# mLSTM stage of a two-layer hybrid block: where modulation sums, a head's norm and the layer norm's squares are worked

## The reference

```python
def even_mixer(h, hc, w_in, w_out, ...):
    p = h @ w_in                                   # and pc = hc @ w_in
    q, k, v, o, g = mlstm_inputs(p, gate_b)
    h_m, hc_m = bidir_mlstm(qc, kc, vc, gc, q, k, v, g)
    y = concat([conv_module(p[..., :2 * D_CONV], ...), mlstm_merge(h_m, o, norm_g)]) @ w_out

def conv_module(glu_in, dw_w, ln_g, ln_b):         # 31 taps, then a layer norm, then silu
    a, b = split(glu_in);  u = dwconv(a * sigmoid(b), dw_w)
    return silu(layer_norm(u, ln_g, ln_b))

def mlstm_merge(h, o, norm_g):                     # RMS norm of each head, times the output gate
    return rms_norm(h, norm_g) * sigmoid(o)
```

## Time and profile before

| | |
|---|---|
| median of three runs | 1645.91 us (1640.68 to 1647.05) |
| the profiled execution | 1644.94 us, its span 1643.2 us, mean granted clock 0.988 |
| busy: PE, PEld, DVE, ACT, POOL | 1602.0, 1346.5, 1022.0, 561.7, 18.1 us |
| taps on DVE, both loops | about 90 to 243 us |
| product `o` on PE, the conv mean in its middle | 251.3 to 273.7 us |
| the heads on PE | 273.7 to 372.7 us |
| `out0` on PE from | 372.7 us |

### The profile page before, as it was taken

One profiled execution on the slowest core, in us unless ns is written; L12 is line 12 of the kernel. 1 busy time (PEld: TensorE's weight loads), 2 busy tenths in 40 slices (PEclk: granted clock), 3 DMA queues, 4 the chain that ended last, 5 costly groups with the idle time before them and its releaser, 6 DMA issues.

```text
span 1643.2 us, 21952 instructions
## 1 busy us (share of the span) xinstructions
PE 1602.0 (97%) x8678; PEld 1346.5 (82%) x8678; DVE 1022.0 (62%) x1505; ACT 561.7 (34%) x896; POOL 18.1 (1%) x58
## 2 busy tenths in 40 slices
PE   6999999999999999999999999899999999999998
PEld 3888887778898888888888887788887988888886
DVE  4999992758847774577526437755876443354345
ACT  5323115465632221132211325523336332232233
POOL 0000000110000000000000000000000000000000
PEclk9999999989999999999999999999999999999999
DMA  9512121434126553445333231220012233223232
GB/s 314 180 28 77 55 75 46 135 103 116 32 73 225 196 178 104 143 164 180 114 97 122 53 101 52 88 96 27 1 31 86 73 94 116 90 90 112 79 97 83
DMA packets 134009, 169.43 MB, mean 103 GB/s; under 512 B 15970, under 2 KB 92450, under 8 KB 133930
## 3 DMA queue, kind: packets, MB, share of 16 engines
q1 hardware_dynamic: 133674, 168.25, 32.0%
q10 hardware_dynamic: 256, 0.08, 0.0%
HBM read 166.17 MB, written 2.15 MB: 102 GB/s over the span
## 4 chain that ended last, share of the span: by engine, by line
PE 91%; DVE 4%; ACT 3%; issue 1%; DMA 1%; SPq 0%; DVEq 0%; POOL 0%; ACTq 0%
PE acc L730 49%; PE acc L779 23%; PE acc L756 4%; PE acc L1191 2%; PE acc L971 2%; PE acc L1122 2%; PE acc L844 2%; PE acc L875 1%; PE acc L1006 1%; PE acc L1137 1%; PE acc L698 1%; DVE h_lo L1649 1%; DVE w_lo L1649 1%; PE acc L950 1%; DMA ada<-in_ada_w 1%
## 5 line engine op out<-in xcount | busy, mean ns | idle before, releaser
L730 PE MATMUL acc<-h_hi,w_hi 128*128 128x512 f32 (+1 forms) x1424 | 417.1, 354 | 4.9 <-DVE w_lo L1649 4.2
L730 PE MATMUL acc<-h_hi,w_lo 128*128 128x512 f32 (+1 forms) x1424 | 412.3, 350 | 0.0
L730 PE MATMUL acc<-h_lo,w_hi 128*128 128x512 f32 (+1 forms) x1424 | 412.1, 350 | 0.0
L1649 DVE TENSOR_TENSOR w_lo<-raw,w_hi 128x1024 fp32r<-128x1024 f32 x183 | 218.2, 1220 | 155.5 <-ACT w_hi L1211 155.3
L730 PEld LDWEIGHTS acc<-h_hi,w_hi 128*128 128x128 f32 x1424 | 230.7, 189 | 42.9 <-issue 5.3
L730 PEld LDWEIGHTS acc<-h_lo,w_hi 128*128 128x128 f32 x1424 | 230.7, 189 | 38.8 <-issue 0.5
L1211 ACT ACTIVATE w_hi<-raw 128x1024 fp32r<-128x1024 f32 x183 | 186.5, 1054 | 216.5 <-PE acc L779 169.9
L730 PEld LDWEIGHTS acc<-h_hi,w_lo 128*128 128x128 f32 x1424 | 229.7, 188 | 37.6
L779 PE MATMUL acc<-w_hi,hid_hi 128*128 128x512 f32 x440 | 175.0, 398 | 0.0
L779 PE MATMUL acc<-w_lo,hid_hi 128*128 128x512 f32 x440 | 174.4, 396 | 0.0
L779 PE MATMUL acc<-w_hi,hid_lo 128*128 128x512 f32 x440 | 174.4, 396 | 0.0
(11 more groups left out here) (267 smaller groups left out, 2057.9 us busy)
## 6 DMA issues: line engine op xcount, KB each, us to landing
ada_w<-in_ada_w SPq DMA_DIRECT2D x88, 512.0 KB, 5.9
raw<-in_ffn_w_in SPq DMA_DIRECT2D x88, 512.0 KB, 3.7
raw<-in_ffn_w_out SPq DMA_DIRECT2D x44, 512.0 KB, 4.2
raw<-in_even_w_in SPq DMA_DIRECT2D x24, 512.0 KB, 4.5
ada<-in_ada_w SPq DMA_DIRECT2D x8, 1024.0 KB, 11.8
raw<-in_odd_w_in SPq DMA_DIRECT2D x12, 512.0 KB, 4.2
raw<-in_even_w_out SPq DMA_DIRECT2D x8, 512.0 KB, 5.4
ada_m<-in_ada_w SPq DMA_DIRECT2D x8, 512.0 KB, 4.2
```

What stands on the lines that cost most here:

```text
L730: last = nc.tensor.matmul(acc[:, s, m, t0:t1], w[:, slot, kk, c], x_[:, k, t0:t1], start=(k == 0 and q == 0), stop=(k == KD - 1 and q == 2))
L1649: return nc.vector.tensor_tensor(out_, in0, in1, op)
```

## The change

- The 1024 columns of `ada_m` become two chunks, `EVEN[2]` and `EVEN[3]`. `EVEN[2]` is summed on DVE in two halves inside the second tap loop (at taps 8 and 16), its columns on PE follow the product `qkov[5]`. `EVEN[3]` is summed after `conv_done`; its columns (`last_columns`, 8 matmuls) come behind item (0, 2) on PE. `ada_m` with its transfers, waits and 128 records goes. On SP the loads of `EVEN[2]` stand ahead of the gates' granules, those of `EVEN[3]` ahead of granules 22 and 23; granules 28 and 29 are loaded after head 0's `negM`.
- The four tiles of squares are added on DVE into one (three additions), so that PE sums one tile. `unit_low(26)` comes after them.
- On ACT, the first exps of head 0 are made before and after the squares, and small activations on one column load the next function's table ahead of need.
- A head's norm is spread over the next head: squares at q = 1 as before, inverse at q = 2, root at q = 3, product at q = 4, turning and gating after q = 5. `head_out` stands after that on ACT, `head_low` at q = 1 of the head after the next on DVE; those of head 2 after the loop. `forward_sums` follows the gating.

```diff
-EVEN = [Chunk((0, 1), q, 0, 4 + q, 0) for q in range(2)]
+EVEN = [Chunk((0, 1), q, 0, 4 + q, 0) for q in range(4)]
...
-ITEMS += [("X", h - 1, 0) if q == "X" else ("S", h, q) for h in range(1, HEADS) for q in (0, 1, 2, "X", 3, 4, 5)]
+ITEMS += [("X", h - 1, 0) if q == "X" else ("S", h, q) for h in range(1, HEADS) for q in (0, 1, 2, 3, 4, 5, "X")]
...
             load_unit(sp, n + 6, w_even, 256)
+            load_ada(sp, 2, 0, 6)
...
                 load_unit(sp, G["qkov"] + 2 * j, w_even, 1024 + 256 * j)
+                if j == 5:
+                    load_ada(sp, 3, 0, 7)
             load_unit(sp, G["o"], w_even, 1024 + 256 * 7)
-            for k in range(4):
+            for k in range(2):
                 load_token(sp, "out0", w_even_out, 0, k)
...
                 if h == 1:
+                    for k in range(2, 4):
+                        load_token(sp, "out0", w_even_out, 0, k)
                     sp.wait_ge(sem("ln_var"), 1)
...
-                load_ada_m(h, h + 1)
...
-                product(pe, U["qkov"] + j, G["qkov"] + 2 * j, h, always)
+                product(pe, U["qkov"] + j, G["qkov"] + 2 * j, h, always, ada=EVEN[2] if j == 5 else None, of=sums_even[0])
...
+            def last_columns():
+
+                pe.wait_ge(ada_used, 4 * EVEN[3].seq + 8)
+                for q in range(4):
+                    for x_ in range(2):
+                        c = 944 + 2 * q + x_
+                        last = nc.tensor.matmul(acc[:, 0, 1, c:c + 1], sums_last[x_][:, q * P:(q + 1) * P], ones[:, 0:1],
+                                                start=False, stop=True, skip_group_check=True)
+                last.then_inc(sem("last_columns"), 1)
...
-                if pending:
+                if kind == "S" and pending:
                     if pending[1] == 0 and hd:
                         pe.wait_ge(sem("sums_taken_fwd"), hd)
                         pe.wait_ge(sem("sums_taken_rev"), hd)
                     weigh(*pending)
-                pending = (hd, q) if kind == "S" else None
+                if kind == "S":
+                    pending = (hd, q)
                 if not z:
-                    spread_sums(lambda t, t0, t1, c: ln_sq[t][:, t0:t1], 1, lambda t: pe.wait_ge(sem("ln_sq_ready"), t + 1)
-                                ).then_inc(sem("ln_var"), 1)
+                    pe.wait_ge(sem("ln_sq_summed"), 1)
+                    for t0, t1 in SEGS[T]:
+                        last = nc.tensor.matmul(acc[:, 1, 1, t0:t1], ones[:, :], ln_sq[0][:, t0:t1], start=True, stop=True)
+                    last.then_inc(sem("ln_var"), 1)
                     psum_free(pe, U["mlstm"] + 1)
-                if kind == "S":
-                    for part in ADA_PARTS.get((hd, q), ()):
-                        ada_part(hd, part)
+                if (kind, hd, q) == ("S", 0, 2):
+                    last_columns()
...
+            def load_table(f, c):
+
+                nc.scalar.activation(mark[:, c:c + 1], eps[:, 0:1], f)
...
+            psum_read(act, U["turned"])
+            sa.done(nc.scalar.activation(gcols[:, 2:4], gcols[:, 2:4], ACT.Exp, scale=-1.0))
+            exps(0, 0, 0, 3)
...
+            exps(0, 0, 3, 4)
+            load_table(ACT.Sigmoid, 12)
...
                     if q == 1 and hd:
-                        finish(hd - 1)
+                        head_squares(hd - 1)
                     if q == 3 and hd:
-                        head_out(hd - 1)
+                        head_root(hd - 1)
...
                                              ).then_inc(sem("sums_taken_rev"), 1)
+                        if hd:
+                            head_out(hd - 1)
...
+                    if (t, w) in ((2, 8), (2, 16)):
+                        ada_sums(EVEN[2], sums_even[0], first=0 if w == 8 else 4, end=4 if w == 8 else KD)
...
             nc.vector.tensor_copy(mark[:, 2:3], ident[:, 0:1]).then_inc(sem("conv_done"), 1)
-            unit_low(26)
+            ada_sums(EVEN[3], [x_[:, :] for x_ in sums_last])
...
+            for t in range(1, 4):
+                sd.wait()
+                dve.wait_ge(sem("ln_sq_ready"), t + 1)
+                ins = vt(ln_sq[0][:, :], ln_sq[0][:, :], ln_sq[t][:, :], ALU.add)
...
+            unit_low(26)
...
+            def head_end(z, hd):
+
+                if hd < HEADS - 1:
+                    dve.wait_ge(sem("slot_full"), z + 2)
+                    weighted(z + 1, hd + 1, 0, 0, 2)
+                forward_sums(hd)
...
                                                    qkov[:, 12 + hd, :], ALU.mult, ALU.mult).then_inc(sem("merged_ready"), 1)
+                    head_end(z, hd + 1)
                     continue
...
-                if q == 1 and hd:
+                if q == 1 and hd >= 2:
+                    head_low(hd - 2)
+                if q == 2 and hd:
                     head_inverse(hd - 1)
+                if q == 4 and hd:
                     head_normed(hd - 1)
...
+            head_low(last - 1)
             head_inverse(last)
```

More of the change, by code:

```diff
@@ L943, in _ @@
             last.then_inc(unit_done, 1)
[L945 to L952, removed]
             def conv_mean():
@@ L956, in conv_mean @@
                 pe.wait_ge(sem("conv_done"), 1)
-                spread_sums(lambda t, t0, t1, c: conv_t[t][:, c:c + t1 - t0], 0, always).then_inc(sem("ln_mean"), 1)
+                for t in range(4):
+                    for (t0, t1), c in zip(SEGS[T], (HALF, U_CTX)):
+                        last = nc.tensor.matmul(acc[:, 1, 0, t0:t1], ones[:, :], conv_t[t][:, c:c + t1 - t0],
+                                                start=(t == 0), stop=(t == 3))
+                last.then_inc(sem("ln_mean"), 1)
             product(pe, U["o"], G["o"], h, always, amid=conv_mean)
@@ L1437, in _, with exps @@
             unit_high(G["qkov"] + 2 * 6 + 4)
+            def load_table(f, c):
+                nc.scalar.activation(mark[:, c:c + 1], eps[:, 0:1], f)
+            def exps(hd, q, first, end):
+                if q == 0 and not first:
+                    act.wait_ge(sem(f"m_in{hd % 2}"), 16 * (hd // 2 + 1))
+                for e, (d, t0, t1) in STEPS[q][first:end]:
+                    if 16 * hd + e == 3:
+                        act.wait_ge(sem("conv_done"), 1)
+                    if 16 * hd + e >= 4:
+                        act.wait_ge(sem("p_used"), 16 * hd + e - 3)
+                    nc.scalar.activation(probs[e % 4][:, 0:t1 - t0], negM[:, hd % 2, d, t0:t1], ACT.Exp,
+                                         bias=gcols[:, d, ORDER[q], hd + 4 * d:hd + 4 * d + 1]).then_inc(sem("e_ready"), 1)
+            psum_read(act, U["turned"])
+            sa.done(nc.scalar.activation(gcols[:, 2:4], gcols[:, 2:4], ACT.Exp, scale=-1.0))
+            exps(0, 0, 0, 3)
             conv_segs = tuple(zip(SEGS[T], (HALF, U_CTX)))
@@ L1453, in conv_root @@
                 last.then_inc(sem("ln_rooted"), 1)
+                load_table(ACT.Exp, 14)
             def conv_silu(first):
@@ L1484, in head_out @@
                 nc.scalar.activation(h_hi[:, 4 + hd, :], merged[hd][:, :], ACT.Copy).then_inc(sem("mix_high"), 1)
-            def exps(hd, q, first, end):
-                if q == 0 and not first:
-                    act.wait_ge(sem(f"m_in{hd % 2}"), 16 * (hd // 2 + 1))
-                for e, (d, t0, t1) in STEPS[q][first:end]:
-                    if 16 * hd + e == 3:
-                        act.wait_ge(sem("conv_done"), 1)
-                    if 16 * hd + e >= 4:
-                        act.wait_ge(sem("p_used"), 16 * hd + e - 3)
-                    nc.scalar.activation(probs[e % 4][:, 0:t1 - t0], negM[:, hd % 2, d, t0:t1], ACT.Exp,
-                                         bias=gcols[:, d, ORDER[q], hd + 4 * d:hd + 4 * d + 1]).then_inc(sem("e_ready"), 1)
             for kind, hd, q in ITEMS:
                 if kind == "S":
-                    exps(hd, q, 2 if hd and not q else 0, 4)
+                    if hd or q:
+                        exps(hd, q, 2 if not q else 0, 4)
                     if (hd, q) == (0, 0):
```

81 lines of the change are left out of this document (31 added, 50 removed).

## The result

The changed kernel takes 1623.54 us, the median of four runs from 1622.82 to 1626.13; the kernel before took 1643.94 beside it (four runs, 1640.68 to 1647.05). The ratio is 0.9885, 95% interval 0.9869 to 0.9902. Measured two more times it is 0.9891 [0.9871, 0.9910] and 0.9893 [0.9872, 0.9914]. The forecast was 1624, so the time is met to half a microsecond. Part of that is luck. The forecast gain, 22.2 of 1645.91 us, is a ratio of 0.9865 and lies just outside the measured interval: by the ratio the gain is 18.9 us, at most 21.5. The 22.2 were subtracted from a median of three runs that lies 2 us above that of the four. The profiled execution takes 1623.9 us, its span 1621.9, mean granted clock 0.995.

What follows compares the result with a forecast made beforehand. TensorE, busy 97% of the span, bounds the kernel; the mLSTM stage holds removable work, waits and half-clock time. Terms 2.2 - 7.2 - 5.1 - 4.9 - 7.2 = -22.2 us take 1645.91 to 1624 us; range 1618 to 1634.

Steps and rivals of the forecast that it cites:

- A: Ahead of the heads: two more chunks on DVE cost PE +2.2 us, bounds 1.7 to 5.
- The cover: DVE's slack ahead of the heads: 2.8 + 3 us; whatever DVE loses beyond 6 us, PE loses too.
- the stall: PE's wait for unit_low(22) behind the columns of EVEN[2], near 231 us: 0.5 us.
- B: Head 0: squares summed on DVE, ada_m out, last_columns in, gaps closed: -7.2 us.
- C: Heads 1 to 3: norm spread off PE's path and ada_m gone: -5.1, -4.9 and -7.2 us.
- rival 1: Heads: clock falls all the same, from small PE gaps and thin work: +8.5 us, 1632; chance 0.13.
- D: Behind the heads: head_low(2) and head_out(2) move after head 3's sums: 0, up to +1 us.
- The table load: ACT's root at q = 3: load 1.28 us without the skill's 1.38 us drain, which would make 1632.
- The signs: Expected traces: clock 1.0 in heads, h_tok the stage's largest wait; w_lo wait over 1 us near 231 proves wrong.
- Slower (2): Heads: clock stays at its lower level throughout, up to 1689 us, half of it 1657; chance 0.03.
- The front (3): Ahead of the heads: granule 22 or the tap loop late, PE stalls 6.5 us, 1631; chance 0.07.
- Rival 4: Heads 1 to 3: den chain or DVE takes the norm's place, -6 instead of -17.2 us, 1635; chance 0.09.

Runs made afterwards that it cites:

- cover: Sixteen further 512-column DVE passes, results unused, put ahead of EVEN[3]'s sums in the changed kernel; one execution, 1627.59 us.
- norm_only: Kernel before with only the norm spread over the next head, ada_m and the four tiles of squares kept; 1635.26 us, ratio 0.9946.
- squares_4: Changed kernel with the four tiles of squares summed on PE again, without DVE's three additions; 1629.76 us, ratio 0.9915.
- norm_block: Changed kernel with the norm put back as one block behind q = 1, ada_m still gone; 1637.88 us, ratio 0.9977.
- late_out: Changed kernel with head_out moved behind the q = 0 exps of the head after the next, root still at q = 3; 1623.76 us, ratio 0.9890.
- no_den: Changed kernel with the denominators left out and ones in their place, so output is not the reference's; one execution, 1620.27 us.
- thin: Changed kernel with 16 two-column matmuls added at q = 2 of heads 1 to 3; 1633.91 us, ratio 0.9952.
- block_filled: Changed kernel with the norm as one block again, plus 18 unread 120-column matmuls a head where PE then idled; 1635.27 us, ratio 0.9958.

## Why the prediction came out, point by point

**A, +2.9 where +2.2 stood.** The terms that were there hold in this execution: 2.12 us from the columns of `EVEN[2]` at 229.88 to the next matmul at 232.00, that is 1.7 of columns and 0.4 of waiting for `w_lo` (forecast 1.7 and 0.5), no wait for granule 22, `conv_done` at 254.2 (253.9), centring from 268.1 (267.5). The rest stands ahead of the taps and is no effect of the change: the columns of `EVEN[1]` start at 82.47, 0.64 us later than in the kernel before, and in the two other traced executions of the changed kernel (one of each further measurement) at 81.52 and 80.88. Counted from those columns to the first scores A is 193.95 - 191.73 = 2.2 us, as forecast.

Two things in A need mending. The cover was mis-sized: 2.8 + 3 us stood, 3.10 + 0.84 are in the trace, and `cover` lost 3.15 us where 6 us of cover would have lost 1.4. And the stall is not fixed. In the traced execution of the third measurement (1624.85 us) PE comes to the columns of `EVEN[2]` 3.7 us earlier, `w_lo` from DVE only 1.6 us earlier, and PE waits 2.4 us (PE in order of time, and the stretch with the columns as above):

```profile
226.22 1.84 PE L685 MATMUL acc<-ones,ada_c 128*128 128x1 f32 x16
230.43 0.98 PE L717 MATMUL acc<-h_hi,w_hi 128*128 128x512 f32 x2 [2.38 <-DVE w_lo L1652]
```
```profile
227.00:237.00 10.00, 7.62 (x34) 6.61 (x34) 10.00 (x11) 4.04 (x8) 0.00 (x0) 0.66 0.35 107
```

The clock falls there as well. Its first scores come at 276.73 all the same. `norm_only`, whose work ahead of the heads is that of the kernel before, has them at 271.33, 2.2 us ahead of the kernel before, though its `EVEN[1]` columns start at 82.13. So A depends on how fast PE gets through its products: counted from the `EVEN[1]` columns it is 2.2 us between these two slower traces, and 195.85 - 189.20 = 6.7 us between these two faster ones, the wait and the lower clock included. That is more than the 5 that stood as its bound.

**B, -6.7 where -7.2 stood.** From the first scores: variance 1.3, weighing 0 at 2.6 (forecast 2.6), columns over at 11.5 (11.4), the last weighing over at 20.3 (19.8), head 1 at 22.35 (21.7). The 0.65 us that it is late are 0.05 to 0.2 at the hand-offs from one engine to another and 2.1 instead of 1.9 for the den chain; the length before, 29.04 in one view, was put at 28.9 by a start from the chain's. The largest single term, the squares, is confirmed by `squares_4`: 3.87 us. The other terms (`ada_m` out of head 0, `last_columns` in, gaps closed) were not tested singly.

**C, -16.8 where -17.2 stood.** Head by head the counting in pieces held to 0.6 us. Two reasons beside it need mending.

The sum is right, but it has no parts that can be had singly. Over the three heads `norm_block` gains 70.1 - 68.9 = 1.2 us, `norm_only` 6.6, both together 16.8: 9 us belong to neither alone. The ratios of the timed runs give less, 5 to 6 us: they make 3.8 us for `norm_block`, 8.9 for `norm_only` and 17.9 to 18.9 for the change, each known to about 3 us (A and B are in the first and the last). In the kernel before, the norm's chain and the `ada_m` piece lay beside each other, each about 4 us long. With either gone the other still holds PE for that time, once as idle time, once as thin work, and mostly with the slow matmuls behind it. Counting before and after as whole chains gave the right answer; adding up the edits would not have.

The clock's cause was put too narrowly. "Each fall comes on the heels of `ada_m`" was true of the rows, but `norm_block` shows the same fall behind 4.1 us of idle PE, so rival 1's premise (gaps lower it as well) holds for long gaps. It didn't come true in the heads: the gaps left there are 0.15 to 0.89 us, and behind those the clock stayed at 1.00 throughout. The rule of "TensorE: Matmul & The Clock Gate", section "A second HAM failure mode: psum-queue depth-cycling", in the Trainium skill (frequent short idles make the clock swing) is thus not borne out in these stretches.

Head 2's miss (18.65, not 18.1) has its place: the exps of q = 0 come late behind `head_out`. I had let `head_out` cost 0.5 us ahead of q = 1 and nothing inside the weighing of q = 0, which takes 2.97 us there instead of 2.72; `late_out` takes that quarter away and `no_den` shows the same engine next in line. The small waits at q = 1 and q = 2 (0.15 each) came in place of the 0.5.

Of the 0.55 us that head 2 is over, that is 0.25. The step from the scores behind weighing 5 to the next head's weighing takes 2.08 us (334.70 to 336.78) where 1.9 stood, and the last 0.1 are hand-offs.

**D** came out 0.6 us below nothing. That tells nothing: in three executions of the changed kernel this stretch takes 1269.9, 1272.6 and 1270.5 us.

**The table load.** ACT's load takes 1.28 us from 307.53, and the exps follow at 308.82. The 1.38 us of drain that the Trainium skill gives in "ScalarE: Activation LUTs", section "What ACT_TABLE_LOAD costs", are absent here too; had they come, `out0` would have started up to 7.8 us later, by the estimate that the prediction made from that figure.

**The signs.** In the profiled execution all named signs were there but one: `h_tok` is the largest wait by PE's own rows (1.9 of 3.6 us), not by those of its weight loads, where `probs` leads with 10.5 to 3.1. The sign should have named the row that costs time. A wait for `w_lo` near 231 us of over 1 us was to make the prediction wrong; the traced execution of the third measurement has it (2.38), though its time, 1624.85 us, is as forecast.

**The rivals.** Slower (2) did not show: in the heads the clock was 1.00 in all three traces of the changed kernel. The front (3) did not show in the first (a stall of 0.4 us); in the third DVE's part of it is there, the 2.4 us above, and no granule was late. Rival 4 had the den chain right as what is late next, and its size wrong: `no_den` gives it 1.4 us for all heads, since ACT's exps come right behind.

## What to carry to other kernels

When a long chain on other engines and filler work on TensorE lie beside each other, count the stage as one chain before and one after: removing one alone can gain almost nothing (1.2 us here), and both together more than the sum. When such a piece is removed, ask what TensorE does in that time afterwards, because four microseconds of idle time and four of matmuls with two columns both brought the lower clock here. A cover of work on another engine must be counted from the engine's own next wait, and in more than one execution: 6 us on paper were 4 here, and a stall of 0.4 us was 2.4 where PE came sooner. And take the next one late from a run with the bottleneck cut out, not from the size of the bottleneck: the den chain of 2 us a head was worth 1.4 us in four heads.

## What was not expected of the hardware

Adding matmuls can pay for itself: 4.2 us of 120-column matmuls a head in place of 4.1 us of idle time shortened three heads by 4.5 us, through the clock. A thin piece does not always lower the clock: 3.6 us of two-column matmuls did it in two of three heads in `norm_only` and in one of three in `thin`. In head 0 the pieces are half as long: in the kernel before the clock stayed up behind both (1.87 and 1.84 us), in `norm_only` it fell behind the first (1.89 us, at 290.29), and head 0 took 1.7 us more.

PE's pace is not fixed by the clock. From the columns of `EVEN[1]` to those of `EVEN[2]` it takes 147.4 us in nine of eleven traces of kernels with the changed front and 145.3 in two, that of the third measurement and that of `block_filled`. The clock is 1.00 in both, and two records of 512 columns start 0.347 us apart in the one and 0.353 in the other. These two are also the ones in which PE waits 2.4 us for `w_lo`. What sets the pace is open.

The clock explains some of the spread between executions of one kernel. The changed kernel at 227 to 237 us, in the execution with a span of 1621.9 and in one with 1625.2:

```profile
227.00:237.00 10.00, 9.72 (x62) 8.63 (x61) 10.00 (x11) 3.95 (x8) 0.00 (x0) 1.00 0.38 115
```
```profile
227.00:237.00 10.00, 9.71 (x53) 8.58 (x53) 10.00 (x11) 4.19 (x7) 0.00 (x0) 0.83 0.35 107
```

The changed kernel was run again beside the other experiments, for this:

> The changed kernel itself on this chip, for comparison with the following ones: 1623.5 us, 0.9885 of the kernel before.

It took 1626.44 us (1622.94 to 1627.16), ratio 0.9891; a third time 1623.61 (1622.94 to 1626.99), ratio 0.9893. In the execution with the lower clock the one-column matmuls of `EVEN[2]` end and PE waits for `w_lo` just as in the other (0.29 and 0.28 us). The clock fell in one and not in the other, in five of the eleven traces in all; why is open. From these columns to the first scores it takes 46.5 us in the one and 48.0 in the other, so this fall costs 1.5 us. That execution had been 0.9 us ahead at the columns, and 2.7 us of the 3.3 between the two spans lie behind the heads.
